# Two more slots for expert weights in the ring, and six of its loads moved into the output projection

## The chip, the cores and the metric

The kernel runs on one core of a Trainium2 chip. The metric is the device time of one execution in microseconds, the median of the runs. TensorE (PE) does the matmuls, VectorE (DVE) and ScalarE (ACT) the elementwise work, GpSimd (POOL) a little, and SyncE (SP) issues nearly all loads. SP works through its instructions in the order in which they are written: while one of them waits for a semaphore, everything behind it waits too.

## The reference, cut to what matters

One decoder layer over 256 tokens of 2048 features in float32. The change touches its second half: the output projection, the first norm, and a hierarchical mixture of 16 experts.

```python
x <- LN1(alpha * x + W_out(merged))
x <- LN2(alpha * x + HierMoE(x))

def _hier_moe(x, wg_r, bg_r, we_r, be_r, w_gate, w_up, w_down):
    ...                      # one of 4 groups, two of its 4 experts for each token: combine (tokens x 16)
    h = jax.nn.silu(jnp.einsum('td,edf->etf', xt, w_gate)) * jnp.einsum('td,edf->etf', xt, w_up)
    h = h * combine.T[:, :, None].astype(h.dtype)
    return jnp.einsum('etf,efd->td', h, w_down).reshape(B, S, D)
```

w_gate and w_up are 16 x 2048 x 512, w_down is 16 x 512 x 2048: 192 MB of expert weights, each read once.

## The kernel before

**Units.** All large weights come in units of 1 MB (128 partitions of 2048 floats). The input projection, the gates, the branches and the output projection (`w_out`, the sixteen units U1 to U1+15) go through a ring of six raw buffers (`raw`, RAW = 6); ACT writes a rounded copy (`whi`, line 1357), DVE the rest (`wlo`, line 1567), two buffers each, and PE multiplies three times per tile (lines 968 to 970). A load into `raw` waits until DVE has split the unit six before it (`lo_done`).

**The tail of the output projection.** After each four `w_out` units DVE adds alpha times the input row block (`residual(c)`, line 774), reading `xres`, the input loaded again into the place of the merged matrix `acc`. Its sum is `xr`. After the last one come the first norm's statistics, the router's logits, the choice of experts and the slot of each token.

**The experts.** They are worked in eight pairs (PAIRS = 8) with 64 token slots for each expert, and more passes only where an expert has more than 64 tokens. A pair has MU = 24 units: 16 of gate and up weights, 8 of down weights. For each pair PE gathers the tokens (line 401), does gate and up (line 428), two transposes (line 464), the down projection (line 476), and during the next pair scatters the result back (lines 413 and 414). PE adds one to `m_used` when it is through with a unit.

**The ring of expert units.** MRAW = 16 slots (`mraw`, `places`), all in memory that earlier stages have left: four in `o1` and `xhi`, six in `raw`, four in `whi` and `wlo`, two in `o2`. `moe_loads` on SP follows the last `w_out` load. It fills the 16 slots as their places come free (`unit_used` at U1, then `lo_done` for the six in `raw`, then `unit_used` at U1+16 for the last six), then waits for `np_ok`, and from unit 16 on waits before each load for `m_used` to say that the slot's unit has been used. The pairs run as one pair written out, a loop over two pairs at a time, and a last pair written out.

**The accumulator.** `acc`, once the merged matrix is no longer needed, is the sum of alpha times the normed stream and the experts' outputs. DVE sets it up after the slot weights of the first pair: eight operations at line 674 and two at line 679, and the last of these adds one to `acc_ok`. In this kernel only the last two loads (`l2g`, `l2b`, the rows of the second norm, lines 371 and 372) wait for `acc_ok` on SP; they go to places of their own and come after the last expert unit. DVE adds the scattered blocks to `acc` (line 688), and after the last pair computes the second norm.

Of the kernel before, what the change touches and what calls it, by code (L numbers as in the profile page):

```python
# [20 lines left out]
P = 128  # L21
D = 2048
S = 256
T = S // P
# [13 lines left out]
DE = 512  # L38
SLOTS = 64
PASSES = -(-S // SLOTS)  # L40
PAIRS = NE // 2
RC = 32
MRAW = 16
MU = 24
ALPHA = 2 ** 0.25
# [41 lines left out]
def build(nc, A, out):  # L87
# [14 lines left out]
    with ExitStack() as ctx:  # L102
# [119 lines left out]
        xres = at("xres", made["acc"], [P, T, D])  # L222
        assert made["wuv"] + 2048 == made["khT"] + 8192 and made["sP"] == made["qst"] + 2048
        l1g, l1b = at("l1g", made["khT"], [P, D]), at("l1b", made["qst"], [P, D])
        l2g, l2b = at("l2g", made["khT"], [P, D]), at("l2b", made["qst"], [P, D])
# [9 lines left out]
        ysb = at("ysb", places[0], [P, D])  # L235
# [37 lines left out]
        def sems(names):  # L273
# [37 lines left out]
        moe_const, sel_ok, eg_in, eg_out, ed_in, ed_out, pos_ps, np_ok = sems(  # L311
            "moe_const sel_ok eg_in eg_out ed_in ed_out pos_ps np_ok")


        mlanded = [sem(f"mlanded{j}") for j in range(MRAW)]
# [24 lines left out]
        def moe_loads(sp):  # L340
            def load(r, pair, turn):

                slot = r % MRAW
                if turn is not None:
                    sp.wait_ge(m_used, turn)
                dst = mraw[slot][:].unsqueeze(1)
                sp.dma_start(dst, expert_unit(r % MU, pair)).then_inc(mlanded[slot], 16)

            def pair_of(m, r, ahead=0):


                return (m * 2 + r // MU + 2 * ahead + (PAIRS if r % MU >= 4 * QUADS else 0)) % PAIRS

            sp.wait_ge(unit_used, U1)
            for r in range(MRAW):
                if 4 <= r < 4 + RAW:
                    sp.wait_ge(lo_done, U1 + 11 + r - 4)
                if r == 4 + RAW:
                    sp.wait_ge(unit_used, U1 + 4 * QUADS)
                load(r, r // MU, None)  # L360
            sp.wait_ge(np_ok, 3)
            more = sp.value_load(runs[0:1, 2:3], min_val=PAIRS // 2 - 1, max_val=PAIRS // 2 * PASSES - 1)
            with sp.Fori(0, more) as m:
                for r in range(MRAW, 2 * MU):
                    load(r, pair_of(m, r), m * (2 * MU) + r - MRAW + 1)
                for r in range(MRAW):
                    load(r, pair_of(m, r, 1), m * (2 * MU) + 2 * MU + r - MRAW + 1)
            for r in range(MRAW, 2 * MU):
                load(r, PAIRS - 2 + r // MU, more * (2 * MU) + r - MRAW + 1)
            sp.wait_ge(acc_ok, 1)  # L370
            sp.dma_start(l2g[:], A["ln2_g"].to_broadcast([P, D])).then_inc(l2_in, 16)
            sp.dma_start(l2b[:], A["ln2_b"].to_broadcast([P, D])).then_inc(l2_in, 16)

        def moe_pe(pe, residual_T, route):
# [18 lines left out]
            def landed_unit(turn, r):  # L393
                value = 16 * (r // MRAW + 1)
                pe.wait_ge(mlanded[r % MRAW], value if turn is None else value + turn * (16 * (2 * MU // MRAW)))

# [19 lines left out]
            def step(turn, r0, m):  # L416
                def gate_up(q):

                    pe.wait_ge(xg_out, 1 + q + m * 4)
                    for w in range(2):  # L420
                        for a in range(2):
                            landed_unit(turn, r0 + 4 * q + 2 * w + a)
                        for kk in range(4):
                            k = 4 * q + kk
                            for a in range(2):
                                unit = mraw[(r0 + 4 * q + 2 * w + a) % MRAW]
# [6 lines left out]
                def put(c):  # L433
                    if turn is not None:
                        scatter(c, m - 1)
# [31 lines left out]
                for f in range(DE // P):  # L467
                    if f % 2 == 0:
                        pe.wait_ge(ht_out, 1 + f // 2 + m * 2)
                    for a in range(2):  # L470
                        landed_unit(turn, r0 + 4 * QUADS + 2 * f + a)
# [1343 lines left out]
```

## Time and profile before

| | us |
|---|---|
| median of 3 runs | 1382.48 (1380.96 to 1383.47) |
| the profiled execution, its own time | 1383.67 |
| span in its trace | 1381.9 |
| PE busy | 1321.0 (96%) |
| DVE busy | 583.3 (42%) |
| ACT busy | 484.2 (35%) |
| mean granted TensorE clock | 0.986 |

PE's busy share is an average over two regimes. Up to about 885 us the dense projections run and the DMA engines are half used. From about 911 us to 1355 us the experts run, and the DMA engines move about 421 GB/s without a break. The time of the profiled execution is 1.77 us above its span and 1.19 us above the median.

### The profile page before, as it was taken

Reading aid. Unit: us, or ns where it says so; the run is one execution under the profiler, and the core shown is the slowest. Engines: PE = TensorE matmul, PEld = TensorE weight load, DVE = VectorE, ACT = ScalarE, POOL = GpSimd, SP = SyncE. Lnnn points to the kernel's source line nnn. Section 1 sums busy time; section 2 is a strip of 40 time slices with the busy share of each in tenths; the row PEclk is TensorE's granted clock in tenths of the full one; section 3 lists DMA queues with packets and bytes.
Section 4 is the critical chain, followed back from the end, with each engine's and each line's share of the span. In section 5 each row is a group of like instructions: output and inputs, shape, how many; then the busy total and the mean of one; then the engine's idle time right before and its main releaser. Section 6 shows DMA issues by size and latency. Waiting matters only on the chain.

```text
span 1381.9 us, 18267 instructions
## 1 busy us (share of the span) xinstructions
PE 1321.0 (96%) x7247; PEld 967.6 (70%) x7247; DVE 583.3 (42%) x737; ACT 484.2 (35%) x656; POOL 38.9 (3%) x51
## 2 busy tenths in 40 slices
PE   7999999999999999999999999799999999999994
PEld 6998988998888888888888878554454443544431
DVE  4476534445546544545455555552122120221206
ACT  3444334335555534544433433411121120211111
POOL 0000000400000000000100000000000000000002
PEclk9999999999999999999999999889999999999997
DMA  9657556544444446554566677679999999999993
GB/s 310 217 174 258 171 187 202 180 163 153 154 150 152 128 163 196 167 167 157 188 201 220 212 243 304 237 299 421 420 421 422 422 422 421 423 422 422 421 421 151
DMA packets 116513, 364.78 MB, mean 264 GB/s; under 512 B 11432, under 2 KB 17000, under 8 KB 91120
## 3 DMA queue, kind: packets, MB, share of 16 engines
q1 hardware_dynamic: 109712, 358.79, 69.9%
q10 hardware_dynamic: 6752, 5.28, 1.3%
q8 instruction: 37, 0.61, 0.2%
q14 instruction: 12, 0.10, 0.0%
HBM read 361.95 MB, written 2.10 MB: 263 GB/s over the span
## 4 chain that ended last, share of the span: by engine, by line
PE 88%; DMA 7%; DVE 3%; ACT 1%; issue 1%; SPq 1%; DVEq 0%; ACTq 0%
PE main L968 19%; PE main L970 18%; PE main L969 18%; PE main L428 13%; DMA mraw<-in_expert_w_down_dram 6%; PE att L476 6%; PE att L401 4%; PE att L1193 1%; PE att L1161 1%; PE main L413 1%; PE main L414 1%; DMA raw<-in_w_in_dram 1%; PE att L1176 1%; ACT whi L1357 1%; PE att L1212 1%
## 5 line engine op out<-in xcount | busy, mean ns | idle before, releaser
L1567 DVE TENSOR_TENSOR wlo<-raw,whi 128x2048 fp32r<-128x2048 f32 (+1 forms) x141 | 324.2, 2299 | 379.5 <-ACT whi L1357 379.5
L1357 ACT ACTIVATE whi<-raw 128x2048 fp32r<-128x2048 f32 (+1 forms) x141 | 269.5, 1911 | 442.4 <-PE main L970 434.2
L428 PE MATMUL main<-mraw,xg 128*64 128x512 f32 x1024 | 225.0, 594 | 0.0
L968 PE MATMUL main<-whi,xhi 128*128 128x512 f32 (+1 forms) x544 | 203.5, 374 | 1.3 <-ACT uT L1396 1.3
L970 PE MATMUL main<-whi,xlo 128*128 128x512 f32 (+1 forms) x544 | 201.7, 371 | 0.0
L969 PE MATMUL main<-wlo,xhi 128*128 128x512 f32 (+1 forms) x544 | 201.5, 370 | 0.0
L428 PEld LDWEIGHTS main<-mraw,xg 128*64 128x64 f32 x1024 | 71.5, 137 | 136.2 <-issue 134.8
L968 PE MATMUL main<-xhi,whi 128*128 128x256 f32 (+1 forms) x560 | 160.1, 286 | 5.0 <-DVE wlo L1567 5.0
L969 PE MATMUL main<-xlo,whi 128*128 128x256 f32 (+1 forms) x560 | 159.3, 285 | 0.0
L970 PE MATMUL main<-xhi,wlo 128*128 128x256 f32 (+1 forms) x560 | 159.3, 284 | 0.0
L476 PE MATMUL att<-mraw,hT 128*64 128x512 f32 x512 | 113.4, 595 | 9.0 <-DMA mraw<-in_expert_w_down_dram 7.8
L968 PEld LDWEIGHTS main<-whi,xhi 128*128 128x128 f32 x544 | 102.6, 189 | 18.4 <-issue 1.5
L970 PEld LDWEIGHTS main<-whi,xlo 128*128 128x128 f32 x544 | 102.5, 188 | 17.8
L969 PEld LDWEIGHTS main<-wlo,xhi 128*128 128x128 f32 x544 | 102.6, 189 | 17.1
L968 PEld LDWEIGHTS main<-xhi,whi 128*128 128x128 f32 (+1 forms) x560 | 107.7, 192 | 6.5 <-DVE wlo L1567 5.0
L969 PEld LDWEIGHTS main<-xlo,whi 128*128 128x128 f32 (+1 forms) x560 | 107.7, 192 | 0.0
L970 PEld LDWEIGHTS main<-xhi,wlo 128*128 128x128 f32 (+1 forms) x560 | 107.7, 192 | 0.0
L525 ACT ACTIVATE xg<-att,gbT 128x128 f32<-128x128 f32 x128 | 47.3, 466 | 139.0 <-PE att L401 139.0
L476 PEld LDWEIGHTS att<-mraw,hT 128*64 128x64 f32 x512 | 39.0, 137 | 78.2 <-issue 76.6
L688 DVE TENSOR_TENSOR acc<-acc,main 128x512 f32<-128x512 f32 x64 | 41.4, 683 | 86.8 <-PE main L414 67.1
L968 PE MATMUL main<-whi,o 128*128 128x512 f32 x192 | 76.4, 398 | 0.0
L970 PE MATMUL main<-whi,o 128*128 128x512 f32 x192 | 74.9, 390 | 0.0
(310 smaller groups left out, 1335.8 us busy)
## 6 DMA issues: line engine op xcount, KB each, us to landing
raw<-in_w_in_dram SPq DMA_DIRECT2D x96, 1024.0 KB, 5.1
mraw<-in_expert_w_gate_dram SPq DMA_DIRECT2D x64, 1024.0 KB, 21.9
mraw<-in_expert_w_up_dram SPq DMA_DIRECT2D x64, 1024.0 KB, 23.6
mraw<-in_expert_w_down_dram SPq DMA_DIRECT2D x64, 1024.0 KB, 22.5
raw<-in_w_branch_dram SPq DMA_DIRECT2D x24, 1024.0 KB, 5.1
raw<-in_w_out_dram SPq DMA_DIRECT2D x16, 1024.0 KB, 5.2
xin<-in_x_dram SPq DMA_DIRECT2D x4, 512.0 KB, 5.9
xres<-in_x_dram SPq DMA_DIRECT2D x1, 2048.0 KB, 7.7
```

Of the source, the lines that this page charges most:

```text
L401: ins = pe.matmul(att[:, q, k % 4 * P:(k % 4 + 1) * P], xr[:, t, k * P:(k + 1) * P], hot[:, t, :], start=(k % 4 == 0 and t == 0), stop=(t ...
L413: pe.matmul(main[1][:, n % 2, :], rows, yhi[:, c % 2, :], start=True, stop=False)
L414: pe.matmul(main[1][:, n % 2, :], rows, ylo[:, c % 2, :], start=False, stop=True).then_inc(sc_ps, 1)
L428: ins = pe.matmul(main[0][half, w, :], xg[:, k, half], unit[:, kk * DE:(kk + 1) * DE], start=(k == 0), stop=(k == KT - 1))
L476: ins = pe.matmul(att[half, c, :], hT[:, f, half], mraw[r % MRAW][:, c * 512:(c + 1) * 512], start=(f == 0), stop=(f == DE // P - 1))
L525: ins = act.activation(xg[:, k, :], att[:, q, k % 4 * P:(k % 4 + 1) * P], ACT.Identity, bias=gbT[:, KT + k:KT + k + 1], scale=gbT[:, k:k + 1])
L688: dve.tensor_tensor(acc[:, t, cols], acc[:, t, cols], main[1][:, n % 2, :], ALU.add).then_inc(sc_free, 1)
L968: pe.matmul(o, ah, bh, start=start, stop=False, skip_group_check=skip)
L969: pe.matmul(o, ah, bl, start=False, stop=False, skip_group_check=skip)
L970: return pe.matmul(o, al, bh, start=False, stop=stop, skip_group_check=skip)
L1357: act.activation(whi[:, u % SPLIT, 0:n], raw[:, slot, 0:n], ACT.Copy).then_inc(hi_done, 1)
L1567: dve.tensor_tensor(wlo[:, u % SPLIT, 0:n], raw[:, slot, 0:n], whi[:, u % SPLIT, 0:n].bitcast(F32), ALU.subtract).then_inc(lo_done, 1)
```

## The change

- MRAW goes from 16 to 18. The two slots that held `o2` go, and four are new: two in `acc` (the merged matrix's place, slots 4 and 5), one in `khT` and one in `qst` (slots 16 and 17), where `l1g` and `l1b`, the first norm's rows, lie until DVE has set up the accumulator.
- The accumulator is now `out_acc` and lies in `o2`. The same instructions write it.
- The input for the residual goes in four pieces of 512 KB: three into the columns of `xr` that are written later, one into `xres3`. They are issued before U1+4 and not before U1+8.
- Units 0 to 5 of the first pair are issued by SP between the `w_out` loads, two each before U1+7, U1+9 and U1+11.
- Units 6 to 17 follow the last `w_out` load (`first_units`): six wait for `lo_done`, four for `unit_used`, and units 16 and 17 for `acc_ok`. From unit 18 on each load waits for `m_used`.
- Six pairs are written out (FIRST = 6), the seventh is a loop that also carries further passes, the eighth is written out. In the loop SP waits for `pair_done`, which ACT raises after the first pair and after every turn.
- `l2g` and `l2b` go into slots of the ring that the last pair has used, and wait for `m_used` there.
- DVE writes one number of turns (`runs`) and not four.

The core of the diff:

```diff
-MRAW = 16
+MRAW = 18
 MU = 24
+FIRST = PAIRS - 2
...
-        places = [O1, O1 + 8192, made["xhi"], made["xhi"] + 8192]
+        places = [O1, O1 + 8192, made["xhi"], made["xhi"] + 8192, made["acc"], made["acc"] + 8192]
         places += [made["raw"] + (U1 + 10 + j) % RAW * 8192 for j in range(RAW)]
-        places += [made["whi"], made["whi"] + 8192, made["wlo"], made["wlo"] + 8192, O2, O2 + 8192]
+        places += [made[name] + (U1 + 14 + j) % SPLIT * 8192 for j in range(SPLIT) for name in ("whi", "wlo")]
+        places += [made["khT"], made["qst"]]
...
+        def first_units(sp, some):
+            for r in some:
+                if r < 4:
+                    sp.wait_ge(unit_used, U1)
+                elif r < 6:
+                    sp.wait_ge(m_ps, 8)
+                elif r < 6 + RAW:
+                    sp.wait_ge(lo_done, U1 + 11 + r - 6)
+                elif r < 10 + RAW:
+                    sp.wait_ge(unit_used, U1 + 4 * QUADS - 1 + (r - 6 - RAW) // 2)
+                else:
+                    sp.wait_ge(acc_ok, 1)
+                load_unit(sp, r, 0, r)
...
+            first_units(sp, range(6, MRAW))
+            for g in range(MRAW, FIRST * MU):
+                sp.wait_ge(m_used, g - MRAW + 1)
+                load_unit(sp, g % MU, g // MU, g % MRAW)
+            sp.wait_ge(np_ok, 1)
+            turns = sp.value_load(runs[0:1, 0:1], min_val=1, max_val=1 + PAIRS * (PASSES - 1))
+            with sp.Fori(0, turns) as m:
+                sp.wait_ge(pair_done, m + 1)
+                for r in range(MU):
+                    sp.wait_ge(m_used, m * MU + FIRST * MU + r - MRAW + 1)
+                    load_unit(sp, r, (m + FIRST) % PAIRS, (LOOP0 + r) % MRAW)
+            for r in range(MU):
+                sp.wait_ge(m_used, turns * MU + FIRST * MU + r - MRAW + 1)
+                load_unit(sp, r, PAIRS - 1, (LAST0 + r) % MRAW)
+            for j, (dst, name) in enumerate(((l2g, "ln2_g"), (l2b, "ln2_b"))):
+                sp.wait_ge(m_used, turns * MU + FIRST * MU + MU - MRAW + 2 + j)
+                sp.dma_start(dst[:], A[name].to_broadcast([P, D])).then_inc(l2_in, 16)
...
-            for n, (a, b) in enumerate(((0.5, PAIRS / 2), (1.0, PAIRS), (0.5, PAIRS / 2 - 1), (1.0, PAIRS - 1))):
-                dve.tensor_scalar(runs[:, n:n + 1], cnt[:, 0:1], a, float(b), ALU.mult, ALU.add).then_inc(np_ok, 1)
+            dve.tensor_scalar(runs[:, 0:1], cnt[:, 0:1], 1.0, None, ALU.add).then_inc(np_ok, 1)
...
-                    if u == U1 + 8:
-                        sp.wait_ge(m_ps, 8)
-                        sp.dma_start(xres[:], A["x"][0].rearrange("(t p) d -> p t d", p=P)).then_inc(xr_in, 16)
+                    if u == U1 + 4:
+                        sp.wait_ge(unit_used, U1 - 2)
+                        for j in range(4):
+                            sp.dma_start(x_of(j), A["x"][0, :, j * 512:(j + 1) * 512].rearrange("(t p) d -> p t d", p=P)).then_inc(xr_in, 16)
+                    if u in (U1 + 7, U1 + 9, U1 + 11):
+                        first_units(sp, range(u - U1 - 7, u - U1 - 5))
```

**SP in the output projection.** Before, from the first `w_out` load to the fifth expert unit (`mraw_133` is slot 0):

```order
L834 DMA raw<-in_w_out_dram 128x4x512 [waits lo_done] x8
L868 DMA xres<-in_x_dram 128x2x2048 [waits m_ps]
L834 DMA raw<-in_w_out_dram 128x4x512 [waits lo_done] x8
L347 DMA mraw_133<-in_expert_w_gate_dram 128x2048 [waits unit_used]
L347 DMA mraw_134<-in_expert_w_gate_dram 128x2048
L347 DMA mraw_135<-in_expert_w_up_dram 128x2048
L347 DMA mraw_136<-in_expert_w_up_dram 128x2048
L347 DMA mraw_137<-in_expert_w_gate_dram 128x2048 [waits lo_done]
```

After, from the first four `w_out` loads to unit 4 (`mraw_132` is slot 0):

```order
L878 DMA raw<-in_w_out_dram 128x4x512 [waits lo_done] x4
L913 DMA xr<-in_x_dram 128x2x512 [waits unit_used]
L913 DMA xr<-in_x_dram 128x2x512 x2
L913 DMA xres_124<-in_x_dram 128x2x512
L878 DMA raw<-in_w_out_dram 128x4x512 [waits lo_done] x3
L363 DMA mraw_132<-in_expert_w_gate_dram 128x2048 [waits unit_used]
L363 DMA mraw_133<-in_expert_w_gate_dram 128x2048 [waits unit_used]
L878 DMA raw<-in_w_out_dram 128x4x512 [waits lo_done] x2
L363 DMA mraw_134<-in_expert_w_up_dram 128x2048 [waits unit_used]
L363 DMA mraw_135<-in_expert_w_up_dram 128x2048 [waits unit_used]
L878 DMA raw<-in_w_out_dram 128x4x512 [waits lo_done] x2
L363 DMA mraw_136<-in_expert_w_gate_dram 128x2048 [waits m_ps]
```

The input moves ahead of four `w_out` loads, and six expert units stand between `w_out` loads where none stood.

**SP from the last slots to the first reload.** Before, from unit 10 (`mraw_143`) to unit 16, the first that goes into a used slot:

```order
L347 DMA mraw_143<-in_expert_w_up_dram 128x2048 [waits unit_used]
L347 DMA mraw_144<-in_expert_w_up_dram 128x2048
L347 DMA mraw_145<-in_expert_w_gate_dram 128x2048
L347 DMA mraw_146<-in_expert_w_gate_dram 128x2048
L347 DMA mraw_147<-in_expert_w_up_dram 128x2048
L347 DMA mraw_148<-in_expert_w_up_dram 128x2048
L362 TENSOR_LOAD runs [waits np_ok]
L362 ISA x2
L363 UNCONDITIONAL_BRANCH
L363 ISA
L347 ISA [waits m_used]
L347 DMA mraw_133<-in_expert_w_down_dram 128x2048
```

After, from unit 14 (`mraw_146`) to unit 20; units 16 and 17 are `mraw_148` and `mraw_149`:

```order
L363 DMA mraw_146<-in_expert_w_up_dram 128x2048 [waits unit_used]
L363 DMA mraw_147<-in_expert_w_up_dram 128x2048 [waits unit_used]
L363 DMA mraw_148<-in_expert_w_down_dram 128x2048 [waits acc_ok]
L363 DMA mraw_149<-in_expert_w_down_dram 128x2048 [waits acc_ok]
L363 DMA mraw_132<-in_expert_w_down_dram 128x2048 [waits m_used]
L363 DMA mraw_133<-in_expert_w_down_dram 128x2048 [waits m_used]
L363 DMA mraw_134<-in_expert_w_down_dram 128x2048 [waits m_used]
```

Unit 16 waited for `m_used` before and waits for `acc_ok` now, and what waits for `m_used` stands behind it.

**DVE where `acc_ok` is raised.** Before, the end of the first pair's slot weights, the ten operations of the accumulator, and what follows:

```order
L645 TENSOR_SCALAR pos<-pos 128x2x2 [waits cmb_ok]
L674 SCALAR_TENSOR_TENSOR acc<-xr,l1g 128x512 [waits z_ok,l1_in]
L674 SCALAR_TENSOR_TENSOR acc<-xr,l1g 128x512 x7
L679 SCALAR_TENSOR_TENSOR acc<-l1b,acc 128x2048 [waits dch]
L679 SCALAR_TENSOR_TENSOR acc<-l1b,acc 128x2048
L683 TENSOR_LOAD runs [waits np_ok,acc_ok]
```

After, the same place:

```order
L680 TENSOR_SCALAR pos<-pos 128x2x2 [waits cmb_ok]
L709 SCALAR_TENSOR_TENSOR out_acc<-xr,l1g 128x512 [waits z_ok,l1_in]
L709 SCALAR_TENSOR_TENSOR out_acc<-xr,l1g 128x512 x7
L714 SCALAR_TENSOR_TENSOR out_acc<-l1b,out_acc 128x2048 [waits dch]
L714 SCALAR_TENSOR_TENSOR out_acc<-l1b,out_acc 128x2048
L666 TENSOR_SCALAR hot<-iota_162,pos,sel 128x64 [waits ws_t,acc_ok]
```

The ten operations stand in the same place behind the same work; the load of a register behind them is gone.

## Rows read from the trace of the kernel before

**Rows 1.** The page's second part: the span in 40 slices of 34.5 us.

```profile
DMA  9657556544444446554566677679999999999993
GB/s 310 217 174 258 171 187 202 180 163 153 154 150 152 128 163 196 167 167 157 188 201 220 212 243 304 237 299 421 420 421 422 422 422 421 423 422 422 421 421 151
```

**Rows 2.** Windows: start and end, length, each engine's busy time, clock, DMA share, GB/s.

```profile
core 0: us, PE busy (x) PEld busy (x) DVE busy (x) ACT busy (x) POOL busy (x), PEclk, DMA share, GB/s
885.00:888.00 3.00, 1.36 (x16) 0.85 (x8) 2.97 (x4) 0.04 (x1) 0.00 (x0) 1.00 0.67 221
888.00:901.00 13.00, 4.89 (x24) 3.79 (x25) 8.84 (x56) 8.59 (x11) 0.00 (x0) 0.51 1.01 427
904.00:909.00 5.00, 5.00 (x28) 2.88 (x29) 5.00 (x6) 2.10 (x6) 0.00 (x0) 0.88 0.00 0
910.00:912.00 2.00, 2.00 (x12) 0.64 (x10) 1.97 (x2) 0.00 (x0) 0.00 (x0) 1.00 0.52 111
930.00:1350.00 420.00, 404.14 (x2066) 182.28 (x2062) 73.35 (x154) 71.07 (x186) 0.00 (x0) 1.00 1.01 421
1354.00:1355.00 1.00, 1.00 (x6) 0.17 (x2) 0.00 (x0) 0.71 (x2) 0.00 (x0) 1.00 0.76 303
```

**Rows 3.** Waits of PE from 905 to 1356 us: total us, times, longest.

```profile
PE att L476 <- DMA mraw<-in_expert_w_down_dram: 7.8, 8, 1.3
```

**Rows 4.** Timeline of SP's loads: start, length of the group, line, how many.

```profile
842.29 0.98 SPq L347 DMA_DIRECT2D mraw<-in_expert_w_gate_dram  x2
...
884.73 0.81 SPq L347 DMA_DIRECT2D mraw<-in_expert_w_up_dram  x2
...
909.80 14.23 SPq L347 DMA_DIRECT2D mraw<-in_expert_w_down_dram  x8
```

**Rows 5.** Timeline of DVE from the number of turns to the accumulator.

```profile
897.92 0.34 DVE L624 TENSOR_SCALAR runs<-cnt 128x1 int32<-128x1 f32 x4
898.18 0.97 DVE L631 TENSOR_SCALAR hot<-iota,pos,sel 128x64 f32<-128x64 f32 x4
...
902.48 7.83 DVE L674 SCALAR_TENSOR_TENSOR acc<-xr,l1g 128x512 f32<-128x512 f32 x8
910.34 4.49 DVE L679 SCALAR_TENSOR_TENSOR acc<-l1b,acc 128x2048 f32<-128x2048 f32 x2
```

**Rows 6.** Timeline of PE at the first expert units.

```profile
905.87 7.09 PE L428 MATMUL main<-mraw,xg 128*64 128x512 f32 x32
```

**Rows 7.** Timeline of PE at the transposes of the third, fourth and fifth pairs.

```profile
1051.05 0.83 PE L464 MATMUL main<-ident,hh 128*128 128x128 f32 x4 [1.03 <-DVE hh L696]
...
1107.08 0.83 PE L464 MATMUL main<-ident,hh 128*128 128x128 f32 x4 [1.03 <-DVE hh L696]
...
1162.91 0.83 PE L464 MATMUL main<-ident,hh 128*128 128x128 f32 x4 [1.03 <-DVE hh L696]
```

**Rows 8.** Timeline of the end: SP's last loads, PE's last units, DVE's second norm.

```profile
1326.18 4.11 SPq L371 DMA_DIRECT2D l2g<-in_ln_g_dram  x1
...
1346.57 3.65 PE L476 MATMUL att<-mraw,hT 128*64 128x512 f32 x16 [1.31 <-DMA mraw<-in_expert_w_down_dram]
1351.54 3.65 PE L476 MATMUL att<-mraw,hT 128*64 128x512 f32 x16 [1.32 <-DMA mraw<-in_expert_w_down_dram]
...
1367.50 2.41 DVE L758 SCALAR_TENSOR_TENSOR acc<-acc,bag,l2g 128x512 f32<-128x512 f32 x2
```

**Rows 9.** SP's last eight w_out loads, and the page's DMA issues: count, size, us to landing.

```profile
799.62 42.62 SPq L834 DMA_DIRECT2D raw<-in_w_out_dram  x8
...
mraw<-in_expert_w_gate_dram SPq DMA_DIRECT2D x64, 1024.0 KB, 21.9
...
raw<-in_w_out_dram SPq DMA_DIRECT2D x16, 1024.0 KB, 5.2
...
xres<-in_x_dram SPq DMA_DIRECT2D x1, 2048.0 KB, 7.7
```

More of the change, by code:

```diff
@@ L338, in build @@
         POOL_OUT, DVE_OUT = blocks[:3], blocks[3:]
-        def moe_loads(sp):
[L341 to L372, printed above, removed]
@@ L433, in put @@
                 def put(c):
-                    if turn is not None:
+                    if fixed != 0:
                         scatter(c, m - 1)
@@ L483, in moe_pe @@
             pe.wait_ge(sc_free, 1)
-            step(None, 0, 0)
-            pe.wait_ge(np_ok, 3)
-            more = pe.value_load(runs[0:1, 2:3], min_val=PAIRS // 2 - 1, max_val=PAIRS // 2 * PASSES - 1)
-            with pe.Fori(0, more) as turn:
-                for h in range(2):
-                    step(turn, (h + 1) * MU, turn * 2 + h + 1)
-            step(more, MU, more * 2 + 1)
+            for m in range(FIRST):
+                step(m)
+            pe.wait_ge(np_ok, 1)
+            turns = pe.value_load(runs[0:1, 0:1], min_val=1, max_val=1 + PAIRS * (PASSES - 1))
+            with pe.Fori(0, turns) as m:
+                step(m + FIRST, ("loop", m))
+            step(turns + FIRST, ("last", turns))
             for n, (t, cols) in enumerate(blocks):
@@ L549, in pair_step, with signal_pair @@
                         act.activation(yhi[:, c % 2, :], att[:, c, :], ACT.Copy).then_inc(y_hi, 1)
-            with act.Fori(0, less) as m:
+            def signal_pair():
+                act.activation(warm[:, 0:1], rowok[:], ACT.Copy).then_inc(pair_done, 1)
+            for m in range(FIRST):
                 pair_step(m, False)
-            pair_step(less, True)
+                if m == 0:
+                    signal_pair()
+            act.wait_ge(np_ok, 1)
+            turns = act.value_load(runs[0:1, 0:1], min_val=1, max_val=1 + PAIRS * (PASSES - 1))
+            with act.Fori(0, turns) as m:
+                pair_step(m + FIRST, False)
+                signal_pair()
+            pair_step(turns + FIRST, True)
             act.activation(warm[:, 3:4], rowok[:], ACT.Sqrt)
@@ L737, in scale, with pair_step @@
                                              ALU.mult).then_inc(l2_mul, 1)
-            with dve.Fori(0, less) as m:
+            def pair_step(m):
                 dve.wait_ge(ws_t, 1 + m)
@@ L744, in dve_moe @@
                 put(m)
-            gated(less)
-            final_adds(less)
-            statistics(less, 4 * T - 1)
+            for m in range(FIRST):
+                pair_step(m)
+            dve.wait_ge(np_ok, 1)
+            turns = dve.value_load(runs[0:1, 0:1], min_val=1, max_val=1 + PAIRS * (PASSES - 1))
+            with dve.Fori(0, turns) as m:
+                pair_step(m + FIRST)
+            gated(turns + FIRST)
+            final_adds(turns + FIRST)
+            statistics(turns + FIRST, 4 * T - 1)
             variance(1)
```

86 lines of the change are left out of this document (52 added, 34 removed).

## The prediction

> **What bounds the kernel now.** I read the slices first, then windows, then who waits at the two ends of the last regime. The slices show two regimes: about 150 to 300 GB/s up to slice 27, then 420 GB/s in every slice but the last [rows 1]. In the second regime the DMA engines are full: share 1.01 and 421 GB/s over 420 us, while PE is busy 404 of 420 us [rows 2]. A unit of 1.049 MB at 421 GB/s takes 2.49 us, so the 24 units of a pair take 59.8 us. PE needs less: from the transposes of one pair to those of the next it takes 55.8 to 56.0 us where it finds its data [rows 7]. So PE falls back on the stream of loads as the ring empties, and its only DMA waits are on the down units, 7.8 us in all, the longest 1.3 [rows 3]. The last two groups of down matmuls both wait, 1.31 and 1.32 us [rows 8]. The landing of the last unit therefore sets the end, and PE's last matmuls, the last scatter and the second norm follow at a fixed distance.
>
> That landing can be counted. Sixteen units are on chip when the experts start, and the DMA engines stand still (share 0.00) from 904 to 909 [rows 2]. SP issues unit 16 at 909.80 [rows 4]. In 910 to 912 only 111 GB/s flow [rows 2]: 0.22 MB, worth 0.53 us at 421, so the stream starts in effect at 912.0 - 0.53 = 911.47, 1.67 us after the issue. 176 units remain: 911.47 + 176 x 2.49 = 1349.7, and the two norm rows end at 1354.7. The window from 1354 to 1355 has a DMA share of 0.76 [rows 2], which is that end. PE's last group starts at 1351.54 [rows 8], 1.8 us after the last unit's bytes. So the time is **the start of this stream plus 176 units plus a fixed tail**, and I ask of each edit what it does to the start and to the count.
>
> **Two more slots and units 16 and 17.** Slots 16 and 17 lie where the first norm's rows lie, so their loads wait for `acc_ok`, the last of DVE's accumulator operations. That wait is new, and behind it on SP stand all loads that wait for `m_used`. When does it end? DVE starts the accumulator at 902.48, straight after the slot weights; eight operations take 7.83 us and two more 4.49 us from 910.34, so it ends at 914.83 [rows 5]. The change takes three of four `runs` operations away ahead of it: four stand in the 0.26 us from 897.92 to 898.18 [rows 5], so three are worth 0.20, and `acc_ok` comes at 914.63. SP's reaction lies between 0 and 0.38 us. The upper end is this: PE's first two units are used up half way through its 32 matmuls, at 905.87 + 7.09 / 2 = 909.42 [rows 6], and SP issued unit 16 at 909.80 [rows 4]. So unit 16 is issued between 914.6 and 915.0, where it was 909.80: **4.8 to 5.2 us later**.
>
> How fast does a stream start from rest? The one before took 1.67 us. Another start, at 884.73 [rows 4], moved 221 GB/s x 3 us = 0.66 MB from 885 to 888 [rows 2], worth 1.57 us, so it began in effect at 886.43, after 1.70 us. I take no difference, bounds -0.1 and +0.1. By 915 PE has used four units, so six loads go out at once and the stream doesn't break.
>
> And the count? Before, units 0 to 15 have landed when the stream starts. After, units 0 to 15 have landed too, since 16 and 17 are the first of the new stream. 176 units remain in both. **The two slots take nothing off the count**, they only allow loads to be issued further ahead, which the full DMA engines can't use: a load takes some 22 us from issue to landing [rows 9], so it already waits behind eight others. Sum of this part: +4.8 to +5.2, taken +4.9.
>
> **Six units in the output projection.** They leave SP some 40 us earlier than 842.29 [rows 4]. But the units that had to wait for their places before (six in `raw`, four in the split buffers) wait for the same events now. The last ones are issued at 884.73 in both; before, six units then kept the DMA engines busy to 901 [rows 2, 4], now four do, to about 896. What is won is 5 us more of idle DMA before the experts. Worth: 0.
>
> Could they delay the projection? SP's eight loads lie 42.62 / 7 = 6.1 us apart [rows 9], and a unit is split six periods after its issue, 36 us. It lands after 5.2 us [rows 9]. The most that comes ahead of one now is the input (7.7 us) or two expert units (5.0 us), so 20 us of slack are left. The added waits of SP (`unit_used` at U1-2 and U1, `m_ps`) are over about a microsecond after the `lo_done` that SP waited for just before. Bounds 0 and +0.5, taken 0.
>
> **The loop written out, `runs`, `pair_done`, norm rows.** The fourth pair, which follows a jump back, took 1107.08 - 1051.05 = 56.03 us, the fifth 55.83 [rows 7]: a jump costs PE 0.2 us, in a regime where it waits for loads anyway. Worth 0, bounds -0.4 and 0. [...] The norm rows now wait for PE to have used nine units of the last pair. Before, the first was issued at 1326.18 and DVE needed both at 1367.50 [rows 8], over 40 us for a load of some 25, and two units are the last of the stream in both. Worth 0. ACT's extra signal is one small operation a pair.
>
> **Sum.** The profiled execution took 1383.67 us: 1383.7 + 4.9 = 1388.6. It lay 1.2 us above the median of the three runs, so for the median 1382.5 + 4.9 = **1387.4 us**, +0.35%.
>
> **The rivals.**
>
> *A, the forecast: the stream starts at `acc_ok`.* 1385.5 to 1389.5 with the bounds above and 1 us for the rate, as 421 to 422 GB/s [rows 1] is 0.2% of 438 us. Chance 0.80.
>
> *B, the deeper ring pays.* If units 16 and 17 came in the idle stretch before 909.8, 174 units would remain and the end be 2 x 2.49 = 5.0 us earlier: 1377.5. It decides itself at one point: `acc_ok` would have to come by about 905, but the operations that raise it take 12.3 us and start at 902.48 [rows 5]. Or the repeated PE gap on the down units comes from too few slots: then 7.8 us [rows 3] go, 1374.7. Against that stands a DMA share of 1.01 while PE waits [rows 2]. Chance 0.06 together. The Trainium skill (Perfetto Trace Analysis, section on optimization strategy) reads a gap that repeats on the busiest engine as a sign of too few buffers. By that rule the two slots would bring those 7.8 us; the full DMA engines say that here it's bandwidth.
>
> *C, the late start is absorbed.* If PE and not the stream set the end, 5 us could vanish. PE's last groups do wait, but only 1.3 us each, and PE's own work is 56 of 59.8 us a pair: should PE run a little later in the last pair than I count, or the projection or the router part gain a little, part is lost. 1382.5 to 1385.2. Chance 0.09.
>
> *D, the projection starves.* If a `w_out` load came more than 20 us late behind the new ones, PE would wait for it, 5 us or more: 1392 and above. Chance 0.05.
>
> **How the numbers follow.** The time is A's, 1387.4. The range 1384.0 to 1390.0 holds A and half of C and leaves out B, D and the rest. A measurement of this kernel can tell about 0.2% (2.8 us) from no change. Faster (below 1379.7) is B, 0.06. Same (to 1385.2) is C with a little of A, 0.11. Slower is the rest of A and D, 0.83.
>
> **What would show it.** In the trace after: unit 16 issued near 914.8, right behind DVE's last accumulator operation; DMA share 0 from about 897 to 915; 421 GB/s from 917 to about 1359; PE's waits for down units up from 7.8 to about 12 or 13 us; the last two groups still waiting 1.3 us; the projection unchanged up to 885. I am wrong if unit 16 leaves before 910, if the DMA share in the expert part falls below 1, or if the last down group no longer waits.

## The result

The kernel after the change takes 1390.24 us (median of 4 executions, 1390.2 to 1391.77), and the kernel before it took 1382.53 us beside it: a ratio of 1.0060, with a 95% interval of 1.0048 to 1.0072. That is 7.7 us slower. The prediction was 1387.4 with a range up to 1390.0, so the direction was right and the size was short by 2.8 us, just outside the range.

The profiled execution took 1391.77 us with a span of 1390.0; before it was 1383.67 and 1381.9. The 8.1 us between them can be followed from the front of the program to its end.

**Unit 16.** The timeline of DVE and then that of SP in the kernel after (start us, length, engine, line, names, how many, and in brackets the idle time ahead and what ended it):

```profile
885.41 2.05 DVE L814 SCALAR_TENSOR_TENSOR xr<-xres,main 128x512 f32<-128x512 f32 x2 [7.57 <-PE main L1017]
...
902.98 7.86 DVE L709 SCALAR_TENSOR_TENSOR out_acc<-xr,l1g 128x512 f32<-128x512 f32 x8
...
910.88 4.49 DVE L714 SCALAR_TENSOR_TENSOR out_acc<-l1b,out_acc 128x2048 f32<-128x2048 f32 x2
```

```profile
885.41 0.81 SPq L363 DMA_DIRECT2D mraw<-in_expert_w_up_dram  x2
...
915.40 4.09 SPq L363 DMA_DIRECT2D mraw<-in_expert_w_down_dram  x8
...
1335.33 2.06 SPq L396 DMA_DIRECT2D l2g<-in_ln_g_dram  x1
```

DVE's accumulator ends at 910.88 + 4.49 = 915.37, and SP issues unit 16 at 915.40. Before it was 909.80 [rows 4]. Of these 5.60 us, 0.67 were there already at the last residual addition: it stands at 885.41 now, and at 884.74 before:

```profile
884.74 2.04 DVE L774 SCALAR_TENSOR_TENSOR xr<-xres,main 128x512 f32<-128x512 f32 x2 [7.57 <-PE main L970]
```

The other 4.93 are that unit 16 now stands behind `acc_ok`. They aren't the whole of that wait, because PE came to the experts sooner in this execution. In `e1` below, where SP waits for PE alone, unit 16 leaves 0.13 us behind the middle of PE's first gate and up group (904.41 + 7.09 / 2 = 907.96, issue at 908.09). In the kernel after that group is

```profile
905.21 7.09 PE L455 MATMUL main<-mraw,xg 128*64 128x512 f32 x32
```

so by this estimate unit 16 could have left at 908.9, and `acc_ok` holds it for 6.5 us; PE's group starts 0.66 us sooner than before [rows 6], though the last residual addition is 0.67 later.

**The stream.** Windows of the kernel after (start and end us, length, busy time of PE, PEld, DVE, ACT, POOL, then the granted clock, the DMA share and GB/s):

```profile
909.00:915.00 6.00, 6.00 (x36) 3.06 (x34) 5.96 (x4) 0.69 (x2) 0.00 (x0) 1.00 0.00 0
916.00:918.00 2.00, 2.00 (x12) 0.69 (x10) 0.00 (x0) 0.00 (x0) 0.00 (x0) 1.00 0.82 209
930.00:1350.00 420.00, 398.34 (x2032) 178.96 (x2030) 73.36 (x154) 71.34 (x188) 0.00 (x0) 1.00 1.01 421
...
1360.00:1361.00 1.00, 1.00 (x8) 0.46 (x6) 0.00 (x0) 0.31 (x1) 0.00 (x0) 1.00 0.62 262
1361.00:1362.00 1.00, 1.00 (x8) 0.41 (x6) 0.00 (x0) 0.74 (x2) 0.00 (x0) 1.00 0.49 205
1362.00:1363.00 1.00, 1.00 (x6) 0.17 (x2) 0.00 (x0) 0.74 (x2) 0.00 (x0) 1.00 0.20 82
```

The DMA engines stand still until 915, and from 930 to 1350 they are as full as before, 1.01 and 421 GB/s against the same in [rows 2]. PE is busy 398.3 of the 420 us where it was busy 404.1. By the way of counting used ahead, 209 GB/s x 2 us = 0.418 MB, worth 0.99 us, so the stream starts in effect at 917.0, 1.6 us after the issue (1.67 before). The end looks different: the share falls over three windows (0.62, 0.49, 0.20). Before it went from nearly full to nearly nothing within two microseconds:

```profile
1353.00:1354.00 1.00, 1.00 (x8) 0.37 (x5) 0.00 (x0) 0.74 (x2) 0.00 (x0) 1.00 0.92 385
...
1355.00:1356.00 1.00, 1.00 (x4) 0.49 (x3) 0.00 (x0) 0.74 (x2) 0.00 (x0) 1.00 0.06 25
```

**PE.** Its last two groups of down matmuls in the kernel after, and below them its waits from 905 to 1365 us (line waited at, for what: us in all, times, longest):

```profile
1354.51 3.65 PE L504 MATMUL att<-mraw,hT 128*64 128x512 f32 x16 [1.23 <-DMA mraw<-in_expert_w_down_dram]
1359.58 3.65 PE L504 MATMUL att<-mraw,hT 128*64 128x512 f32 x16 [1.42 <-DMA mraw<-in_expert_w_down_dram]
```

```profile
PE att L504 <- DMA mraw<-in_expert_w_down_dram: 12.7, 12, 1.4
...
PE main L455 <- DMA mraw<-in_expert_w_up_dram: 2.2, 2, 1.1
```

The last group starts at 1359.58 and started at 1351.54 [rows 8]: 8.04 us later, and both still wait for their data. From the issue of unit 16 to this group it takes 1359.58 - 915.40 = **444.18 us**, where it took 1351.54 - 909.80 = **441.74**. So the 8.04 us are 0.67 ahead of 885, 4.93 from there to the start of the stream, and 2.44 in the stream of 176 loads itself. The 0.67 lie in PE's first waits (5.9 us for an input where it waited 5.5, and the like), and belong to the execution: in a second profile of the same kernel (`e10` below) the last residual addition stands at 884.04. There PE's group starts at 904.22 and unit 16 leaves at 913.13, so the same reckoning gives 5.2 us for `acc_ok`. The 2.44 is what the prediction had at nothing, and the experiments are mostly about it.

**What the page lists beside the loads.** Part 3 of the profile's page, one line of before and one of after (packets, MB, share of 16 engines):

```profile
q8 instruction: 37, 0.61, 0.2%
```

```profile
q8 instruction: 46, 0.75, 0.2%
```

These are program code on its way to an engine: 0.61 MB in 37 packets is 16 KB a packet, and the profile counts them against the same 16 DMA engines as the loads. That most of the ones in the stream are PE's is shown by `e3` and `e4` below. In the stretch of the stream alone (909 to 1352 before, 915 to 1360 after) the DMA view counts 8 and 18:

```profile
q8 instruction: 8, 0.13, 0.1%
```

```profile
q8 instruction: 18, 0.29, 0.3%
```

A loop body that is run again need not be fetched again: before, while PE goes round its body of two pairs, this queue has no fetch from 1044 to 1300. In the kernel after, where all pairs of PE stand in a row, one comes every 16 to 39 us.

### The profile page after: what moved, and what is told of

Read it like the earlier page. It is cut to its first block, busy times and chain, and to the rows that moved or that the text cites. A ratio compares the mean times of both kernels' runs of the same rounds, so it can differ in the third digit from the quotient of the medians.

```text
span 1390.0 us, 17633 instructions
## 1 busy us (share of the span) xinstructions
PE 1321.2 (95%) x7247; PEld 965.0 (69%) x7247; DVE 582.8 (42%) x734; ACT 484.3 (35%) x658; POOL 38.9 (3%) x51
## 4 chain that ended last, share of the span: by engine, by line
PE 87%; DMA 8%; DVE 3%; ACT 1%; issue 1%; SPq 0%; DVEq 0%; ACTq 0%
PE main L1015 18%; PE main L1017 18%; PE main L1016 18%; PE main L455 13%; DMA mraw<-in_expert_w_down_dram 8%; PE att L504 5%; PE att L421 4%; PE att L1240 1%; PE att L1208 1%; PE main L433 1%; PE main L434 1%; DMA raw<-in_w_in_dram 1%; PE att L1223 1%; ACT whi L1404 1%; PE att L1259 1%
## 5 line engine op out<-in xcount | busy, mean ns | idle before, releaser
L504 PE MATMUL att<-mraw,hT 128*64 128x512 f32 x512 | 114.5, 596 | 13.4 <-DMA mraw<-in_expert_w_down_dram 12.7
L721 DVE TENSOR_TENSOR out_acc<-out_acc,main 128x512 f32<-128x512 f32 x64 | 41.4, 683 | 87.2 <-PE main L434 67.2
```

What stands on the lines that cost most here:

```text
L504: ins = pe.matmul(att[half, c, :], hT[:, f, half], src[:, c * 512:(c + 1) * 512], start=(f == 0), stop=(f == DE // P - 1))
L721: dve.tensor_tensor(out_acc[:, t, cols], out_acc[:, t, cols], main[1][:, n % 2, :], ALU.add).then_inc(sc_free, 1)
```

## The experiments

Theory **F** (fetch): ten more fetches take turns on the DMA engines and make one engine's share of the loads late; a unit has landed when the slowest of the 16 has delivered. Rival **S** (slots): the new places, the six early loads or the longer ring cost the time. Rival **R** (run): nothing but the spread from one execution to the next. Times are medians; each ratio is against the kernel before, run beside it.

### Slots and loop apart

`e1` keeps the change but has 16 slots, so that no load waits for `acc_ok`:

```
-MRAW = 18
+MRAW = 16
-        places += [made["khT"], made["qst"]]
```

> The changed kernel without slots 16 and 17 (16 slots; unit 16 waits for m_used and nothing on SP waits for acc_ok). If the wait for acc_ok starts the stream late (4.9 us of the 7.7), unit 16 leaves near 910.5 and the time is about 1390.2 - 4.9 = 1385.3. If the deeper ring is worth something, it is above 1390. If the rest (about 2.5 us) is in the instructions that writing out six pairs adds, it stays: the last down group still starts about 2.5 us later behind the stream's start than before, and the page still shows some 46 fetches of 16 KB.

Measured: 1384.51 us, ratio 1.0010 (1.0001 to 1.0018). The kernel after is 5.7 us above it. Of the kernel's own +7.7 us, then, most leaves with the two slots and about 2 stay. SP's timeline and PE's last group in `e1`:

```profile
908.09 9.80 SPq L362 DMA_DIRECT2D mraw<-in_expert_w_down_dram  x6
```

```profile
1352.16 3.65 PE L503 MATMUL att<-mraw,hT 128*64 128x512 f32 x16 [1.32 <-DMA mraw<-in_expert_w_down_dram]
```

From issue to last group it is 1352.16 - 908.09 = 444.07 us, as in the kernel after (444.18), with 16 slots as with 18. The 2.4 us don't come from the slots.

`e4` is `e1` with PE's loop back in its place (one pair, a loop over two pairs run three times, the last pair). SP, ACT and DVE stay written out. Further passes of the experts are left out of `e2` and `e4`.

```
-            for m in range(FIRST):
-                step(m)
...
-            with pe.Fori(0, turns) as m:
-                step(m + FIRST, ("loop", m))
+            step(0)
+            with pe.Fori(0, 3) as t2:
+                for h in range(2):
+                    step(t2 * 2 + (h + 1), ("two", h, t2))
+            turns = 1
             step(turns + FIRST, ("last", turns))
```

> Both: 16 slots, and PE as in the kernel before (one pair, a loop of three turns of two pairs, one pair; further passes left out on PE). What is left of the change is the six loads in the output projection, the accumulator's place, SP, ACT and DVE written out. If the late start and the fetches are the whole of the loss, the time is that of before, 1382.5 within 1 us. If moving the six loads gains anything, it is below 1381.5; if the moved loads cost, above 1384.

Measured: 1382.08 us, ratio 0.9994 (0.9986 to 1.0003), 2.4 us under `e1`, from PE's loop alone. Its SP and PE rows:

```profile
908.55 9.80 SPq L362 DMA_DIRECT2D mraw<-in_expert_w_down_dram  x6
```

```profile
1350.34 3.65 PE L507 MATMUL att<-mraw,hT 128*64 128x512 f32 x16 [1.31 <-DMA mraw<-in_expert_w_down_dram]
```

1350.34 - 908.55 = 441.79 us, the number of the kernel before (441.74), and the stream sees 8 fetches. A second queue of fetches (q14, 8 KB each) has 6 in this stretch in the kernel after and 6 in `e4` too, so it isn't the cause. Everything else in the change (six early loads, the accumulator's place, three fewer `runs` operations, the other engines' loops written out, later norm rows) is in `e4` and together costs nothing that can be measured.

`e3` goes the other way: the kernel before, with the first two turns of PE's loop written out.

```
-            with pe.Fori(0, more) as turn:
+            for turn in range(2):
+                for h in range(2):
+                    step(turn, (h + 1) * MU, turn * 2 + h + 1)
+            with pe.Fori(2, more) as turn:
```

> The kernel before, but PE's second to fifth pairs are written out and not looped, nothing else. Theory fetch: some 9 to 10 fetches of 16 KB more, the spread between DMA engines grows from 2.3 to 3.3 or 4.8 us, and the time from 1382.5 to 1383.5 - 1385. Rival (places or depth of the ring): no change, 1382.5.

Measured: 1384.32 us, ratio 1.0011 (1.0002 to 1.0020): 1.8 us for this edit alone, with about 1.2 us of uncertainty. Its rows:

```profile
908.30 9.81 SPq L347 DMA_DIRECT2D mraw<-in_expert_w_down_dram  x6
```

```profile
1352.59 3.65 PE L476 MATMUL att<-mraw,hT 128*64 128x512 f32 x16 [1.31 <-DMA mraw<-in_expert_w_down_dram]
```

1352.59 - 908.30 = 444.29 us, with 18 fetches. So the same 2.4 us can be taken out of the kernel after and put into the kernel before by PE's loop alone; S falls for them, and R with it.

`e2` is the kernel after with a PE loop that fits 18 slots, two turns of three pairs:

```
+            step(0)
+            with pe.Fori(0, 2) as t3:
+                for h in range(3):
+                    step(t3 * 3 + (h + 1), ("three", h, t3))
+            turns = 1
             step(turns + FIRST, ("last", turns))
```

> The changed kernel, but PE runs the second to seventh pairs as a loop of two turns of three pairs, so its program is three pairs shorter; SP, ACT, DVE and all 18 slots as changed. Further passes for experts with more than 64 tokens are left out on PE; these inputs have none. Theory fetch: each 16 KB instruction fetch holds up one of the 16 DMA engines by about 1.5 us, fetches go round the engines, and a unit has landed only when the slowest engine has. Then some 8 fetches fewer take the spread between the engines from 4.9 to 2 or 3 us and the time to 1387.5 to 1389 (one lap of 1.5 us, or the whole 2.5). Rival: the 2.5 us come from the new places or from the depth of the ring; then it stays at 1390.2 although the fetches are fewer.

Measured: 1391.88 us, ratio 1.0059 (1.0042 to 1.0075): nothing was won. Its page and PE's waits say why:

```profile
q8 instruction: 48, 0.79, 0.2%
```

```profile
PE main L433 <- issue: 4.4, 1, 4.4
```

A body of three pairs is fetched again, 48 fetches and not fewer, and at the jump back PE stands still for 4.4 us. The expectation asked for fewer fetches and got none fewer, so its numbers can't be held against either theory. But the run tells a loop from its fetches. PE's last group:

```profile
1359.09 3.65 PE L508 MATMUL att<-mraw,hT 128*64 128x512 f32 x16 [1.29 <-DMA mraw<-in_expert_w_down_dram]
```

Unit 16 is issued at 913.65, so the stream takes 445.44 us with 20 fetches in it: PE runs a loop here and the stream is as long as where PE is written out, or longer. PE's stop of 4.4 us isn't the reason, for the earliest of the 16 engines is through as soon as in the other kernels (434.7 us, see below). It's the fetches that cost, and not the written-out form. The run also shows the limit of the remedy: two pairs are kept on chip and three are not.

### Where in the stream the time is lost

Each load raises its semaphore 16 times, by one for each DMA engine's share, and PE waits for all 16. The traces keep the time of each of these steps. For the last unit before they lie between 1349.14 and 1351.41, and PE's last group starts at 1351.54; after it is 1354.56 to 1359.44, and PE at 1359.58. PE starts 0.13 and 0.14 us behind the slowest share. The table takes, for the last unit, how far the slowest share lies behind the earliest (the lag). At the first unit it is 0.3 to 0.6 us in every kernel. `e5` to `e11` are told further down.

```
kernel   16 KB     units in   unit 16 issued -> last     the same for   slowest engine behind
         fetches   stream     down group, us             176 units      earliest at last unit, us
before      8       176         441.74                     441.74          2.3
e4          8       176         441.79                     441.79          2.5
e5          8       175         439.29                     441.78          2.4
e11         8       175         438.95                     441.44          1.9
e1         17       176         444.07                     444.07          4.8
after      18       176         444.18                     444.18          4.9
e10        18       176         444.24                     444.24          5.1
e3         18       176         444.29                     444.29          4.9
e9         18       174         439.92                     444.90          5.7
e8         18       176         445.10                     445.10          5.2
e2         20       176         445.44                     445.44          6.2
e6          8       176         443.76                     443.76          3.4
e7          8       175         440.77                     443.26          2.6
```

(2.49 us are added for each unit that a kernel's stream has less than 176.) Where the first pair runs as before, eight fetches give 441.4 to 441.8 and seventeen to twenty give 444.1 to 445.4, whatever the slots, places and waits are. `e6` and `e7`, which change the first pair, stand apart with 8 fetches and 443.3 to 443.8; they have gaps in the loads of that pair, see below. The earliest share needs the same time from the first unit to the last in before, `e3`, `e4`, `e1` and after, 434.7 to 434.9 us; only the slowest differs, 436.8 against 439.1 to 439.3. So the memory and the rate are not slower: one or a few engines are late. That is the ragged end in the windows above.

The lag grows in steps of about 1.5 us, and each step stands beside a fetch. In the kernel after it goes from 0.5 to 1.9 us at the load that comes in around 923, beside the stream's first fetch (921.9); from 1.8 to 3.3 at the load that comes in from 1126.0 to 1129.3, beside the ninth (1126.7); and from 3.3 to 4.8 at the one from 1322.3 to 1327.1, beside the seventeenth (1324.8). `e1`, `e3`, `e9` and `e10` have their steps at the first, ninth and seventeenth fetch too, and `e8` at the second, tenth and eighteenth. The fetches between hardly raise the lag. That fits fetches which are dealt to the engines in a fixed order and come back to the slowest one with every eighth; the records name no engine, so it is an inference. By it the cost goes by rounds and not by the number of fetches: eight fetches hit the slowest engine once, seventeen or eighteen three times.

The DMA view of 1125 to 1140 shows what one fetch takes:

```profile
q1 hardware_dynamic: 863, 6.29, 100.8%
q8 instruction: 1, 0.02, 0.5%
```

0.5% of 16 engines over 15 us is 1.2 us of one engine for 16 KB (the share is rounded; the record itself says 1.0 to 1.1). Why a share is delayed by 1.5 us and not by 1.1, the records don't show.

### How much the wait for `acc_ok` is worth

`e8` adds two operations of DVE ahead of `acc_ok` in the kernel after, with a factor of zero:

```
+            for t in range(T):
+                ins = dve.scalar_tensor_tensor(out_acc[:, t, :], l1b[:], 0.0, out_acc[:, t, :], ALU.mult, ALU.add)
             ins.then_inc(acc_ok, 1)
```

> The changed kernel with two more DVE operations of 2.25 us ahead of acc_ok (they add zero times a row to the accumulator). If acc_ok starts the stream, each microsecond there is one at the end: 1390.2 + 4.5 = 1394.7. Rival: if SP's wait is not what counts, 1390.2.

Measured: 1396.01 us, ratio 1.0102 (1.0087 to 1.0118): 5.8 us above the kernel after by the medians, with some 2 us of uncertainty. In its profile:

```profile
913.09 4.49 DVE L717 SCALAR_TENSOR_TENSOR out_acc<-l1b,out_acc 128x2048 f32<-128x2048 f32 x2
```

```profile
917.62 4.95 SPq L363 DMA_DIRECT2D mraw<-in_expert_w_down_dram  x8
```

```profile
1356.14 3.65 PE L504 MATMUL att<-mraw,hT 128*64 128x512 f32 x16 [1.23 <-DMA mraw<-in_expert_w_down_dram]
1362.72 3.65 PE L504 MATMUL att<-mraw,hT 128*64 128x512 f32 x16 [2.92 <-DMA mraw<-in_expert_w_down_dram]
```

SP again leaves 0.04 us behind DVE's last operation. The wait decides the start of the stream, and what is added there arrives at the end in full. That is best seen against `e10`, whose last residual addition stands at the same place (884.04, here 884.02): unit 16 leaves 4.49 us later, and the last group starts 5.35 us later (1362.72, there 1357.37). The last group waits 2.92 us here, 1.5 more than in the kernel after. The lag rises from 3.7 to 5.2 us at the last load but one, and the eighteenth fetch is recorded at 1357.5, while that load comes in: the third step fell on the last two loads, where in the kernel after it had fallen 30 us ahead of them. That is the 0.9 us by which this stream is longer.

`e9` gives the two slots a place that is free in time. The loads of the first norm's rows and their use are left out (the ten operations read `xr` in place of the rows, so the output isn't the layer's), and with them SP's wait:

```
                 else:
-                    sp.wait_ge(acc_ok, 1)
...
-            sp.dma_start(l1g[:], A["ln1_g"].to_broadcast([P, D])).then_inc(l1_in, 16)
-            sp.dma_start(l1b[:], A["ln1_b"].to_broadcast([P, D])).then_inc(l1_in, 16)
```

> The changed kernel with slots 16 and 17 free from the start: the first norm's rows are left out (neither loaded nor multiplied and added; the accumulator is set up by the same ten operations from the normed stream alone), so units 16 and 17 wait for nothing but the six units before them. What the two slots would be worth if they were free: the stream starts at about 909 to 910 and has 174 units, so 1390.2 - 5.5 - 5.0 = 1379.7, about 5 us under e1_sixteen_slots (1384.5). Rival: PE ends the kernel then, and the time stays near 1382 to 1384.

Measured: 1379.69 us, ratio 0.9975 (0.9966 to 0.9984). Against `e1` (1384.51) two more units ahead of the stream bring 4.8 us, as 2 x 2.49 = 5.0 says, and 174 units remain. The same two slots that bring nothing behind `acc_ok` are worth 5 us where they can be filled in the idle stretch. This was rival B's own condition, and its price was right. Against the kernel before `e9` gains 3.1 us and not 5, because it keeps the 18 fetches.

### A version that beats both

The kernel before has the room for one unit: the place of `qbT` is free when the experts begin. `e5` loads unit 10 there once and shifts the ring so that unit 16 goes out with the first sixteen:

```
+        once = at("once", made["qbT"], [P, UNIT])
...
-            for r in range(MRAW):
+            for r in range(MRAW + 1):
...
+                if r == 10:
+                    sp.dma_start(once[:].unsqueeze(1), expert_unit(10, 0)).then_inc(once_in, 16)
+                else:
+                    slot = r + 1 if r < 10 else r % MRAW
+                    sp.dma_start(mraw[slot][:].unsqueeze(1), expert_unit(r, 0)).then_inc(mlanded[slot], 16)
```

> The kernel before with one place more, for one unit only: unit 10 of the first pair goes into the 8 KB of the place that holds yhi and ylo from the end of the first pair on, and unit 16 into the place that unit 10 had, at once, without waiting for PE; units 17 to 26 then each wait for the unit 17 before them. Places that are free before 909 us are what counts: 17 units have landed, 175 remain, the stream starts when it did, so 1382.5 - 2.5 = 1380.0. Rival: it makes no difference because PE's own pace ends the kernel (1382.5).

Measured: 1379.71 us, ratio 0.9980 (0.9971 to 0.9989). SP's timeline shows the extra unit and unit 16 in the idle stretch, and the stream then starts as late as before, with one unit less:

```profile
884.87 0.33 SPq L364 DMA_DIRECT2D once<-in_expert_w_up_dram  x1
...
887.97 0.44 SPq L367 DMA_DIRECT2D mraw<-in_expert_w_down_dram  x1
909.78 12.76 SPq L350 DMA_DIRECT2D mraw<-in_expert_w_down_dram  x7
```

It beats the kernel before by 2.6 us and, in the pair of runs below, the kernel after by 10.7.

`e6` tries to start the stream sooner instead: in the kernel before, PE takes the first gate and up block of the first pair ahead of the second gather.

```
                 gather(0)
+                if turn is None:
+                    gate_up(0)
                 put(1)
```

> The kernel before, but in the first pair PE does the first quarter of gate and up straight after the first gather and the second gather behind it, so units 0 and 1 are used up some 2.3 us sooner and the stream of loads starts by that much sooner. If the start of the stream sets the end: 1382.5 - 2.3 = 1380.2, less if PE, which runs at half clock there, does the matmuls at that clock. Rival: 1382.5.

Measured: 1383.74 us, ratio 1.0013 (1.0004 to 1.0022): no gain, and 3.5 us over the 1380.2 expected. The stream did start sooner, unit 16 at 906.72 where it leaves at 907.93 to 909.80 in the profiles whose first pair is unchanged and that don't wait for `acc_ok`. Two windows of the first pair show what came next:

```profile
912.00:920.00 8.00, 8.00 (x45) 3.67 (x46) 1.35 (x1) 2.91 (x8) 0.00 (x0) 1.00 0.96 380
...
925.00:930.00 5.00, 5.00 (x26) 1.63 (x24) 0.59 (x3) 0.00 (x0) 0.00 (x0) 1.00 0.98 388
```

PE is busy all the time and gives slots back more slowly than 421 GB/s fills them, so the stream that started sooner runs at 380 and 388, where it ran at 426 and 428 before. The earliest share needs 435.8 us to the last unit, 1.0 more than before, and the lag is 3.4 and not 2.3: together these are the 2.0 us by which the stream is longer (443.76 and 441.74). The releases in the first pair are a second bound just behind the first. Why the lag rose at the third fetch here, and why the median is even above that of the kernel before, is not shown. `e7` joins the edits of `e5` and `e6`:

> Both edits of e5_one_more_place and e6_first_gate_early: 1382.5 - 2.5 - 2.3 = 1377.7 if the two add, as they should if the end is the start of the stream plus the units that remain. Rival: 1380, if PE becomes the bound.

Measured: 1381.49 us, ratio 0.9994 (0.9985 to 1.0003), a miss: 3.8 us over the 1377.7 expected and worse than `e5` alone. Here too the loads of the first pair come with gaps: 405 GB/s from 925 to 930 and 383 from 930 to 935.

The kernel after and `e5` were run once more side by side:

> The changed kernel itself once more, beside the next one on the same chip and in more rounds: 1390.2 within 1 us. If it falls to 1388.7 or less, the part of its loss above the forecast (2.5 us) was in the chip or the rounds and not in the kernel.

> The kernel of e5_one_more_place once more, since it is the only one that beats both kernels with the right output: 1379.7 to 1380.2, 2.5 us under the kernel before and some 10 us under the changed one. If it is within 1 us of the kernel before, its gain was luck of the first rounds.

Measured: 1389.85 us, ratio 1.0057 (1.0043 to 1.0071), and 1379.17 us, ratio 0.9979 (0.9970 to 0.9988). Both first results stand. In `e10` unit 16 is issued at 913.13, 2.3 us sooner than in the first profile of the same kernel, and from there to the last group it takes 444.24 us again: the start of the stream moves from one execution to the next, its length hardly does. `e5` and `e11` are one kernel too, with the start at 909.78 and 907.93 and lengths of 439.29 and 438.95.

## Why the prediction was short

- **What bounds the kernel**: right. With the same bytes and the same 421 GB/s, the end follows the issue of unit 16 (forecast A). Both last groups wait, 1.23 and 1.42 us. The signs that it named came: DMA share 0 up to 915, unit 16 at 915.40, 12.7 us of waits for down units.
- **`acc_ok`**: the mechanism right, the size a little low. Forecast 4.8 to 5.2, taken 4.9. SP's reaction is 0.03 us, and `e8` shows that the wait arrives at the end in full. By the medians, after less `e1`, it is 5.7 us, and within one profile 6.5 and 5.2. The 4.9 was taken from a single profile in which PE came to the experts late: unit 16 left 25.06 us behind the last residual addition (909.80 - 884.74), in `e1` 23.86 (908.09 - 884.23). That the two profiles differ by 4.93 at this place is in part luck.
- **The count of 176 units**: right, and the reason too: `e9`, which frees the places in time, gains the 5 us that the kernel after doesn't. The other half of rival B, that PE's repeated wait for down units comes from too few slots, is refuted: with two slots more the waits grew from 7.8 to 12.7 us (forecast 12 to 13).
- **Six units in the projection, the wait of SP's queue, norm rows, `runs`**: taken 0; `e4`, which has them all, is at 0.9994.
- **The loop written out**: this step failed. It was costed by the jump that it saves PE, "Worth 0, bounds -0.4 and 0", and what the code costs to fetch was left out. The profile's page of the kernel before has the line with 37 fetches, and the prediction didn't use it. At the jump that it priced nothing was fetched: between 1044 and 1300 this queue is empty. It measured +1.8 (`e3`), +2.4 (`e1` less `e4`) and +2.4 (the stream in the profile). With it the sum is 1382.5 + 4.9 + 2.4 = 1389.8, against 1390.2; the 0.4 left over is less than `acc_ok` was short by.
- **The fixed tail**: this is where the missing term acts. The prediction counted the last unit's bytes to 1349.7 and took the 1.8 us from there to PE's last group as fixed. They are the lag of the slowest share (1351.41) and 0.13 us, and the lag went from 2.3 to 4.9 us.
- **The range**: it allowed 1 us for the rate of the stream. The rate did hold; what moved is when the slowest engine ends, which no row of rates shows. With the fetches at nothing, 1390.0 was too low by 0.24 us.

The Trainium skill (Runtime: NRT & Kernel Launch, section on instruction fetch mechanics) calls the cost of crossing a 16 KB block of code "mostly hidden". For PE that holds here: from 905 to 1365 us the kernel after shows no wait of PE for its own issue. For a stream of loads that already fills the DMA engines it doesn't hold: ten blocks more cost 2.4 us. The measurement decides. The same section says that kernels prefer full unrolling, because a taken branch breaks the sequential prefetch and, where its target isn't among the pages held, forces a fetch. On these loads the loop of two pairs is the cheaper form, and its jumps fetched nothing; the loop of three pairs, which is fetched again and stalls 4.4 us, fits what the section says.

## What to carry to other kernels

Where DMA is the bound, count the bytes that remain when the last wait before the stream ends; a buffer helps only if it can be filled before that point (2.5 us a unit here), and not if its place comes free later than the one it joins. When an edit writes a loop out, look at the instruction fetches on the profile's page: here they rode on the same DMA engines as the data, and a load that was spread over all of them landed with the slowest. And put such a stream's first load behind nothing but its own buffer: what stood on the queue behind `acc_ok` paid for it in full.

## What the runs showed of the hardware that was not expected

- A 16 KB instruction fetch takes 1.0 to 1.1 us of one DMA engine, and in a full stream the lag of the slowest share grows by about 1.5 us at a time, at every eighth fetch in the six profiles with 17 or 18 of them. 8 fetches left 1.9 to 2.6 us between the earliest and the slowest share at the end (3.4 in `e6`), 17 to 20 left 4.8 to 6.2.
- PE's body of two pairs runs again without being fetched (no fetch on q8 from 1044 to 1300); a body of three pairs is fetched again (20 fetches in the stream) and costs 4.4 us at the jump.
- The granted clock of PE between 888 and 905, while it waits much for the router, differs from one execution to the next: 0.50 before (the lower of its two levels, 1.2 GHz, all the time), 0.60 in the kernel after, but also 0.51 in `e5` and 0.60 in `e11`, which are one kernel. PE's first gate and up matmul stands 19.80 us behind the last residual addition in the kernel after and 21.13 before [rows 6], which is a part of what moves the start of the stream. The windows, of before and of after:

```profile
888.00:905.00 17.00, 8.89 (x43) 7.79 (x44) 12.73 (x66) 10.10 (x15) 0.00 (x0) 0.50 0.79 332
```

```profile
888.00:905.00 17.00, 8.99 (x53) 7.65 (x52) 12.72 (x64) 10.10 (x15) 0.00 (x0) 0.60 0.31 116
```

What stays open: why the clock came back sooner in one than in the other, which engine each fetch goes to, and what nine to sixteen fetches in the stream would cost, for no kernel here has them.
